# Projecting q and k of the differential layers transposed, in halves of the columns, in a four-layer decoder trunk

## What is computed

```
def diff_attention(h, w_in, w_out, lam, subln_g, cos, sin, lambda_init):
    proj = h @ w_in
    q, k, v, g = jnp.split(proj, [nq, 2 * nq, 2 * nq + DA_WIDTH], axis=-1)
    q = rope(q.reshape(B, S, 2 * H, d), cos, sin) * (d ** -0.5)
    k = rope(k.reshape(B, S, 2 * H, d), cos, sin)
    ...
        s = jnp.einsum('bhmqd,bhmkd->bhmqk', qblk, k, preferred_element_type=jnp.float32)
        p = jax.nn.softmax(jnp.where(mask, s, NEG), axis=-1)
        pd = p[:, :, 0] - lam_full * p[:, :, 1]
        return jnp.einsum('bhqk,bhkv->bhqv', pd.astype(v.dtype), v, preferred_element_type=jnp.float32)
```

## Time and profile before

| | |
|---|---|
| median of 3 runs | 1755.6 us |
| the profiled execution | 1755.62 us |
| its span | 1753.9 us |
| TensorE busy | 1745.0 us (99%) |
| VectorE busy | 1142.6 us (65%) |
| ScalarE busy | 911.0 us (52%) |
| granted TensorE clock, mean | 0.999 |

### The profile page before, as it was taken

How to read it: one execution, slowest core, us unless ns; L and a number is a source line. 1 busy time by engine, 2 the same in 40 slices (tenths; PEclk the granted TensorE clock), 3 DMA queues, 4 the chain that set the end, 5 groups by cost and what they waited for, 6 DMA issues and landing times.

```text
span 1753.9 us, 24994 instructions
## 1 busy us (share of the span) xinstructions
PE 1745.0 (99%) x8274; PEld 1458.5 (83%) x8274; DVE 1142.6 (65%) x1890; ACT 911.0 (52%) x1420; POOL 40.1 (2%) x99
## 2 busy tenths in 40 slices
PE   9999999999999999999999999999999999999998
PEld 8888888888888888888888888888888888888887
DVE  7766666665558888865655465655666666666655
ACT  7554545454556666645544444454545445454543
POOL 1000000000000000000000000000000000000000
PEclk9999999999999999999999999999999999999999
DMA  8666566655565555457997699766666666656563
GB/s 274 188 178 180 170 183 171 184 167 191 181 183 165 158 157 156 152 180 166 171 167 205 175 170 180 203 171 191 181 186 176 179 179 172 186 169 181 172 212 131
DMA packets 171300, 313.16 MB, mean 179 GB/s; under 512 B 10870, under 2 KB 27836, under 8 KB 171100
## 3 DMA queue, kind: packets, MB, share of 16 engines
q1 hardware_dynamic: 170800, 311.54, 64.8%
q0 software_dynamic: 48, 0.13, 0.2%
q10 hardware_dynamic: 380, 0.56, 0.1%
HBM read 310.10 MB, written 2.10 MB: 178 GB/s over the span
## 4 chain that ended last, share of the span: by engine, by line
PE 98%; DMA 1%; SPq 1%; DVE 0%; issue 0%; ACT 0%; POOLq 0%; POOL 0%; DVEq 0%
PE acc L957 30%; PE acc L959 30%; PE acc L958 30%; PE tp L922 4%; DMA raw<-in_da_w_in_dram 1%; PE sc L958 1%; PE sc L957 1%; PE sc L959 1%; PE sc L989 0%; PE sc L1047 0%; PE sc L1045 0%; PE sc L1046 0%; PE sc L1028 0%; PE sc L1027 0%; PE sc L1115 0%
## 5 line engine op out<-in xcount | busy, mean ns | idle before, releaser
L1770 DVE TENSOR_TENSOR w_lo<-raw,w_hi 128x1024 fp32r<-128x1024 f32 x583 | 708.1, 1223 | 463.8 <-ACT w_hi L894 462.5
L894 ACT ACTIVATE w_hi<-raw 128x1024 fp32r<-128x1024 f32 x583 | 613.5, 1058 | 456.5 <-PE acc L959 454.6
L957 PE MATMUL acc<-w_hi,xt_hi 128*128 128x512 f32 x1824 | 719.6, 394 | 0.2 <-DVE w_lo L1770 0.2
L959 PE MATMUL acc<-w_hi,xt_lo 128*128 128x512 f32 x1824 | 711.4, 390 | 0.0
L958 PE MATMUL acc<-w_lo,xt_hi 128*128 128x512 f32 x1824 | 710.3, 389 | 0.0
L959 PEld LDWEIGHTS acc<-w_hi,xt_lo 128*128 128x128 f32 x1824 | 342.3, 188 | 72.7
L958 PEld LDWEIGHTS acc<-w_lo,xt_hi 128*128 128x128 f32 x1824 | 342.8, 188 | 65.8
L957 PEld LDWEIGHTS acc<-w_hi,xt_hi 128*128 128x128 f32 x1824 | 342.6, 188 | 66.0 <-DVE w_lo L1770 0.3
L957 PE MATMUL acc<-w_hi,ot_hi 128*128 128x512 f32 (+1 forms) x520 | 202.6, 390 | 0.0
L959 PE MATMUL acc<-w_hi,ot_lo 128*128 128x512 f32 (+1 forms) x520 | 201.0, 386 | 0.0
L958 PE MATMUL acc<-w_lo,ot_hi 128*128 128x512 f32 (+1 forms) x520 | 200.7, 386 | 0.0
(11 more groups left out here) (287 smaller groups left out, 1136.6 us busy)
## 6 DMA issues: line engine op xcount, KB each, us to landing
raw<-in_da_w_in_dram SPq DMA_DIRECT2D x255, 512.0 KB, 3.7
raw<-in_ml_w_in_dram SPq DMA_DIRECT2D x96, 512.0 KB, 5.1
raw<-in_sw_w_in_dram SPq DMA_DIRECT2D x72, 512.0 KB, 3.7
raw<-in_da_w_out_dram SPq DMA_DIRECT2D x64, 512.0 KB, 3.7
raw<-in_sw_w_out_dram SPq DMA_DIRECT2D x32, 512.0 KB, 3.6
raw<-in_ml_w_in_dram SPq DMA_DIRECT2D x64, 256.0 KB, 4.5
raw<-in_ml_w_out_dram SPq DMA_DIRECT2D x32, 512.0 KB, 3.9
xres<-in_x_dram SPq DMA_DIRECT2D x3, 512.0 KB, 8.8
```

The costliest lines, as they stand in the source:

```text
L894: act.activation(w_hi[:, q:q + 2, :], raw[:, 2 * p:2 * p + 2, :], ACT.Copy).then_inc(hi_ready, 1)
L957: pe.matmul(out_ap, k_hi, m_hi, start=start, stop=False)
L959: return pe.matmul(out_ap, k_lo, m_hi, start=False, stop=stop)
L1770: dve.tensor_tensor(w_lo[:, two, :], raw[:, two, :], w_hi[:, q:q + 2, :].bitcast(F32), ALU.subtract).then_inc(lo_ready, 1)
```

## The change

In the differential layers the roles are exchanged for q and k: the weights are stationary (128 columns), and the moving operand is the x of all 256 tokens, high and low part side by side (`xt`, 512 wide) for the high part of the weights, and the high part of x alone (256 wide) for the low part. The result is q or k already transposed, heads' dimensions by tokens. The left half of a bank collects high x high and low x high, the right half high x low. ScalarE copies the right half to SBUF, and VectorE adds the left half. The job is done in two halves of 256 columns: pairs 0 to 3 hold all 2048 rows of the first half (1 KB pieces in memory), pairs 4 to 7 those of the second. The first q job of the program keeps its load order, and both halves end with pair 7.

The rotary tables are scaled by the tokens' norm factor and transposed by TensorE once per layer, since tokens now run along the row; the rotary step works on 64 partitions at a time for its cross terms. In the third layer the 256-wide fp32 score becomes three passes, with operands that are split when they are copied.

```
-ITER_EMPTIED_BY = {"da": ["act", "act", "dve", "dve"], "sw": ["act", "dve"], "ml": ["act", "dve", "act", "dve"]}
+ITER_EMPTIED_BY = {"da": ["dve", "dve", "dve", "dve"], "sw": ["act", "dve"], "ml": ["act", "dve", "act", "dve"]}
...
-DA = dict(q_evac=11, q_T=10, q_copy=14, k_evac=19, k_T=18, k_copy=22, v_evac=27,
+DA = dict(sums=(7, 11, 15, 19), table=10, table_T=8, table_copy=13, rope=(14, 16, 18, 20), split_hi=(15, 17, 19, 21),
+          split_lo=(15, 17, 19, 21), v_evac=27,
...
-        xt_hi, xt_lo = sb("xt_hi", [P, KC, S], F32R), sb("xt_lo", [P, KC, S], F32R)
+        xt = sb("xt", [P, 2, KC, S], F32R)
+        xt_hi, xt_lo = xt[:, 0], xt[:, 1]
...
+            def load_halves(w, col, J):
+
+                half = JW // 2
+                for p in range(PAIRS):
+                    sp.wait_ge(pairs_done, PAIRS * J + p + 1 - PAIRS)
+                    row, a = 4 * P * (p % 4), p // 4
+                    sp.dma_start(raw[:, 2 * p:2 * p + 2, :].rearrange("p c (b n) -> p (c b) n", b=2),
+                                 w[row:row + 4 * P, bass.ds(col + half * a, half)].rearrange("(k p) n -> p k n", p=P))\
+                      .then_inc(raw_full[p], 16)
...
-                if (i := w.due(DA["q_evac"])) is not None:
-                    evac(l, job(i, 0), i, par, qs)
...
+                for n in range(4):
+                    half, whole = n % 2, (q_whole, k_whole)[n // 2]
+                    if (i := w.due(DA["sums"][1 if w.start and n == 0 else n])) is not None:
+                        if w.start and n == 0:
+                            act.wait_ge(first_half, 1)
+                        else:
+                            act.wait_ge(pairs_done, PAIRS * job(i, n // 2) + 4 * half + 4)
...
-                if (i := w.due(DA["q_T"])) is not None:
-                    pe.wait_ge(sig["roped"], in_iter(l, "roped", i, 2))
-                    turn_eight(lambda t: qs[:, t, :], [in_iter(l, f"tp_{b}", i, 0) for b in range(2)])
-                if (i := w.due(DA["k_T"])) is not None:
-                    pe.wait_ge(sig["roped"], in_iter(l, "roped", i, 4))
-                    turn_eight(lambda t: ks[:, t, :], [in_iter(l, f"tp_{b}", i, 1) for b in range(2)])
+                if w.phase == "iter" and w.first and w.idx == DA["table_T"]:
+                    pe.wait_ge(sig["table"], in_head(l, "table", 1))
...
-                        pe.matmul(sc[h][:, 0:S], kT[:, h, 0:P], qT[:, h, :], start=True, stop=True)
+                        three(sc[h][:, 0:S], ml_k0_hi[:, h, :], ml_k0_lo[:, h, :], ml_q_hi[:, h, :], ml_q_lo[:, h, :], True, True)
...
+            def column(bank, m, k, hi, lo):
+
+                a = lambda stop: pe.matmul(acc[bank][m][:], hi, xt[:, :, k, :], start=k == 0, stop=stop)
+                b = lambda stop: pe.matmul(acc[bank][m][:, 0:S], lo, xt_hi[:, k, :], start=False, stop=False)
...
+            def pair_of_half(w, j0, j, p, par, b):
...
+                for c in range(4):
+                    k = 4 * (p % 4) + c
+                    if w.first_job_of_layer and k in (0, 12, 14):
+                        for name in ("tp_0", "tp_1") if k == 0 else ("tp_0",) if k == 12 else ("tp_1",):
+                            pe.wait_ge(free[name], in_out(w.l - 1, name, 4 if k else 3))
+                    for m in range(2):
+                        op = column(b, m, k, hi[:, c, P * m:P * m + P], lo[:, c, P * m:P * m + P])
...
+            def q_or_k_pair(w, j0, i, j, p):
+
+                par = LOOP0[w.l] % 2
+                half = p // (PAIRS // 2)
+                if p % (PAIRS // 2) == 0:
+                    if j == 1:
+                        wait_half_emptied(pe, w.l, j0 - 1, half, i)
+                    elif not w.first:
+                        wait_emptied(pe, w.l, j0 + 2 + half, i - 1)
...
+            def turn_half(s, before):
...
+                own.step(dve.tensor_tensor(a, s, cos_t, ALU.mult))
+                low, high = slice(0, 64), slice(64, P)
+                own.step(dve.tensor_tensor(b[low], s[high], sin_t[high], ALU.mult))
+                own.step(dve.tensor_tensor(b[high], s[low], sin_t[low], ALU.mult))
+                own.wait()
+                dve.tensor_tensor(s, a, b, ALU.add).then_inc(sig["roped"], 1)
...
+                        for m in range(2):
+
+                            part = whole[:, 2 * half + m, :]
+                            dve.wait_ge(sig["low_part"], in_iter(l, "low_part", i, 2 * n + m + 1))
+                            op = dve.tensor_tensor(part, part, acc[(par + half) % 2][m][:, 0:S], ALU.add)
+                        op.then_inc(dve_emptied, 1)
```

More of the change, by code:

```diff
@@ L80 @@
     "x_sq":      ((0, 0, 8), (0, 0, 8), (0, 0, 8), (0, 0, 8)),
+    "table":     ((0, 0, 0), (1, 0, 0), (0, 0, 0), (0, 0, 0)),
+    "qk_lo":     ((0, 0, 0), (0, 4, 0), (0, 0, 0), (0, 0, 0)),
+    "low_part":  ((0, 0, 0), (0, 8, 0), (0, 0, 0), (0, 0, 0)),
     "roped":     ((0, 0, 0), (0, 4, 0), (2, 2, 0), (0, 0, 0)),
@@ L407, in build, with wait_half_emptied @@
         block = ctx.enter_context(nc.Block())
+        first_half = sem("first_half")
+        def wait_half_emptied(eng, l, j, half, i):
+            eng.wait_ge(dve_emptied, emptied(l, j, i)[1] - 1 + half)
         def wait_emptied(eng, l, j, i=0):
@@ L499, in iteration @@
                                 load_first(w_in)
+                            elif j < 2:
+                                load_halves(w_in, D * j + JW * i, J + j)
                             else:
@@ L841, in side_ml @@
                 if (i := w.due(ML["qk_copy"])) is not None:
-                    take(qT[:, 0:2, :], "tp_0", tp[0][:], in_iter(l, "tp_0", i, 0))
+                    act.wait_ge(full["tp_0"], in_iter(l, "tp_0", i, 1))
+                    act.activation(ml_q_hi[:, 0:2, :], turned(0), ACT.Copy).then_inc(sig["qk_hi"], 1)
+                    act.wait_ge(full["tp_1"], in_iter(l, "tp_1", i, 1))
+                    act.activation(ml_k0_hi[:, 0:2, :], turned(1)[:, :, 0:P], ACT.Copy).then_inc(sig["qk_hi"], 1)
                 for h in range(2):
@@ L1164, in pair @@
                 if p == 0:
-                    if w.phase == "iter" and not w.first and j < 2:
+                    if w.kind == "da" and w.phase == "iter" and j == 2:
+                        wait_half_emptied(pe, w.l, j0 - 1, 0, i)
+                    elif w.phase == "iter" and not w.first and j < 2:
                         wait_emptied(pe, w.l, j0 + ITER_JOBS[w.kind] - 2, i - 1)
@@ L1447, in side_da @@
[L1447 to L1456 removed]
+                if w.phase == "iter" and w.first and w.idx == DA["table"]:
+                    dve.wait_ge(rstd_ready, 2 * l + 1)
+                    for t in range(T):
+                        scale = rstd[:, t:t + 1]
+                        halves = rope_rows[:, t].rearrange("p x (a n) -> p x a n", a=2)
+                        dve.tensor_scalar(halves[:, 0], cos_a[:, t, :].unsqueeze(1).to_broadcast([P, 2, 64]), scale, None,
+                                          ALU.mult)
+                        for a in range(2):
+                            op = dve.tensor_scalar(halves[:, 1, a], sin_a[:, t, 1 - a, :], scale, None, ALU.mult)
+                    op.then_inc(sig["table"], 1)
@@ new lines, in side_da @@
+                for n in range(4):
+                    job, half, whole = LOOP0[l] + n // 2, n % 2, (q_whole, k_whole)[n // 2]
+                    two = slice(2 * half, 2 * half + 2)
+                    at = DA["sums"][1 if w.start and n == 0 else n]
+                    if (i := w.due(at)) is not None:
+                        for m in range(2):
+                            part = whole[:, 2 * half + m, :]
+                            dve.wait_ge(sig["low_part"], in_iter(l, "low_part", i, 2 * n + m + 1))
+                            op = dve.tensor_tensor(part, part, acc[(par + half) % 2][m][:, 0:S], ALU.add)
+                        op.then_inc(dve_emptied, 1)
+                    if (i := w.due(DA["rope"][n])) is not None:
+                        if w.first:
+                            dve.wait_ge(free["sc_0"], in_head(l, "sc_0", 1))
+                        wait_half_emptied(dve, l, job, half, i)
+                        turn_half(whole[:, two, :], in_iter(l, "roped", i, n))
+                    if (i := w.due(DA["split_lo"][n])) is not None:
+                        hi, lo, src = ((q1_hi, q1_lo, q_whole[:, two, P:S]), (kT_hi, kT_lo, k_whole[:, two, :]))[n // 2]
+                        dve.wait_ge(sig["qk_hi"], in_iter(l, "qk_hi", i, n + 1))
+                        dve.tensor_tensor(lo[:, two, :], src, hi[:, two, :].bitcast(F32), ALU.subtract)\
+                           .then_inc(sig["qk_lo"], 1)
@@ L1670, in side_ml @@
                 if (i := w.due(ML["qk_copy"])) is not None:
-                    take(kT[:, 0:2, :], "tp_1", tp[1][:], in_iter(l, "tp_1", i, 0))
+                    for b, (whole, hi, lo, cols) in enumerate(((ml_q1, ml_q_hi, ml_q_lo, slice(0, S)),
```

(6 more changed lines are left out.)

117 lines of the change are left out of this document (77 added, 40 removed), and 6 rows, old and new, of the table COUNTS.

## The result

The changed kernel takes 1758.42 us (median of 20 runs, 1756.61 to 1760.66); the kernel before, on the same chip, 1755.68 us (20 runs, 1755.11 to 1757.51). The ratio is 1.0014, 95% interval 1.0008 to 1.002. So it is **slower by 2.7 us**, by less than 0.2% but with an interval that leaves no change out, where 6.5 us faster was forecast and nothing above 1752.5 was in the range.

What follows compares the result with a forecast made beforehand. TensorE was taken as the bound, busy 1745.0 of 1753.9 us. Terms -14.4 + 4.8 + 0.9 - 0.6 + 2.8 = -6.5 took 1755.6 to 1749.1 us, range 1746.0 to 1752.5.

Steps and rivals of the forecast that it cites:

- Transposes removed: Differential layers: 16 blocks of eight q and k transposes go, 0.9 us each, -14.4 us.
- Projection with the weights stationary: Differential q and k jobs: a 512-wide plus a 256-wide matmul, 0.2266 + 0.118 us, cost slightly more than before; +4.8 us.
- Rival A: q and k projections: alternating widths cost a weight load, slower from 0.128 us per 256-wide matmul, 1821 at 0.188; chance 0.06.
- The wait at the start: First k job: TensorE waits for ScalarE's copies and VectorE's adds, behind older work, to empty bank 0; +2.8 us, ends 0.4 and 4.
- Tables: Four rotary-table transposes once per differential layer, half a block each time; +0.9 us.
- third layer's scores: Third layer: 256-wide fp32 score of 0.43 us becomes three passes of 0.118, eight times; -0.6 us.
- fourth layer's start: Fourth layer's first job reads xt columns 12 to 15 already in pair 3; no cost, 1.1 us to spare.
- transfers: q and k loads come as 1 KB pieces; no cost, 10.9 us of cover.
- VectorE and ScalarE off the path: Differential iterations: VectorE gets 3.3 us more work, but neither engine delays TensorE in the steady state; no cost.
- B: No change: TensorE also waits 0.5 us per differential iteration for q's or k's halves, 4 at the start; 1754.3 us, chance 0.08.
- D: Removed transposes had covered work TensorE then waits for, half of the 14.4 comes back; 1756.3 us, chance 0.02.
- C: The wait at the first k job is absorbed as slower pairs relieve VectorE's chain; 1746.3 us, chance 0.08.

Runs made afterwards that it cites:

- all-512 version: The version with the later tables, with the low weights against both parts of x, so every q and k matmul is 512 wide; a price measurement only: 1857.35 us.
- The run with the dummies: Changed kernel with 18 unused fp32 matmuls of 128 columns ahead of TensorE's wait at the first k job: 1756.24 us.
- two and two: The version with the later tables, with both 512-wide matmuls of each k first, then both 256-wide ones: 1751.03 us.
- eight and eight: The version with the later tables, with all eight 512-wide matmuls of a pair, then its eight 256-wide ones (reversed where a half ends): 1750.91 us.
- the version with the later tables: Changed kernel with the rotary table steps moved to pairs 11 and 12 and the first half's copies and adds to pair 10: 1752.87 us.

## Why the prediction was wrong

The sign is wrong: -6.5 forecast, +2.7 measured. By its own steps:

- **Transposes removed, -14.4:** right. 1.8 per iteration fits the all-512 version to 0.05.
- **Projection with the weights stationary, +4.8:** this is the step that failed most, and by size. A unit was priced at 0.2266 + 0.118 = 0.3446 and came to 0.3515, so the term to 1024 x (0.3515 - 0.3399) = +11.9. Inside the change the 256-wide step takes 0.1167, as forecast; the 512-wide one was carried over at its price in a run of its own width, 0.2266, and takes 0.2348. In the trace of before, the 512-wide matmul behind the nine of the earlier trace rows already takes 0.23 to 0.24 to the next start (93.81 to 94.05). Prices of runs of one width would not have been enough: 0.2266 for 512 columns less 256 columns at the 2.4 GHz level, 0.1067, is 0.1199, and alone a 256-wide matmul does take 0.1200. With it the term would have been +6.8 and the forecast still -4.5. A matmul in a run of its own width costs its columns and 13 ns more, and that accounts for 2.0 of the 6.9 ns; the other 4.9 are the mixing, which no term had. The Trainium skill (TensorE: Matmul & The Clock Gate, Wait — 56ns, not 53.3ns?) puts the same form, columns over the clock plus a fixed part, with 2.5 ns for the fixed part. The form agrees with the runs of one width, the 2.5 does not: 13.3 is measured at both widths. At the lower level the Trainium skill has no fixed part in that section, and there the trace agrees: 0.42 to 0.43 and 0.21 to 0.22 in the stretch from 40.06. Rival A, that the alternation of widths costs, had the right direction; its turning point, 0.128 for the 256-wide matmul, was not reached (0.3515 - 0.2266 = 0.125, if all is put on it). Its working gives 1749.1 + 1024 x 0.0069 = 1756.2 for the unit that was measured, which is no gain against the kernel before, yet hardly slower; its end at 0.188 is out.
- **The wait at the start, +2.8:** the mechanism, the place and the chain are right, the size is not, 4.2. The run with the dummies compares best, as its sine steps stand where those of the earlier trace rows do. There the six table steps take 1.4 us (34.37 to 35.78), not 0.8; `w_lo` (1.14) and the adds (0.8) came as forecast, and the adds end at 37.7 instead of 37.0. TensorE was ready at 33.8, not 34.4. The two together are the 1.2 to 1.4 that the wait is longer. The prediction had the price of the table steps among its ends: 4 if they cost twice as much, and they cost 1.8 times.
- **What follows the wait:** missing altogether. The sum treated a wait as a delay and nothing else. The granted clock falls during it, and what comes behind pays 2.2 us more. The experiment with the dummies shows that this is the idle time's doing.
- **Tables, third layer's scores, fourth layer's start, transfers:** right, as far as they can be told apart. A score of the third layer now takes 0.36, as three steps from 875.00 to 875.36, instead of 0.43:

```profile
875.00 0.28 PE L996 MATMUL sc<-kT_hi,q_hi 128*128 128x256 f32 x1
...
875.36 0.38 PE L1155 MATMUL sc<-q,k 128*128 128x128 f32 x2
```

  From the first layer's last scores to the fourth layer's first the change gains 0.71. The terms give a gain of 0.43: the 1.8 of one iteration's transposes less 128 x 0.0116 = 1.48 for its units, less 0.45 for the tables, and 0.56 for the scores. So these terms are right within 0.3 us together. The stretches of the changed kernel that answer to the earlier trace rows:

```profile
120.00:175.00 55.00, 55.00 (x299) 47.27 (x298) 42.06 (x61) 24.87 (x36) 0.00 (x0) 1.00 0.62 184
860.00:915.00 55.00, 55.00 (x265) 46.22 (x264) 30.23 (x45) 29.54 (x43) 1.42 (x3) 1.00 0.98 161
```

- **VectorE and ScalarE off the path, rivals B and D:** no wait stands in any iteration, so B and D are out; C is out too, since the wait at the start is there.
- **The Trainium skill's rule on bare weight loads (TensorE: Matmul & The Clock Gate, The mechanism):** out, as the trace of before had it. The steps of 0.2266 in the all-512 version, with a weight load each and the weights stationary, show it for the new form too.

With the measured unit, wait and clock the sum is -14.4 + 11.9 + 0.9 - 0.6 + 4.2 + 2.2 = +4.2, against +4.8 in the profiled execution and +2.7 between the medians. Part of the 2.1 between those two is the late load at the start of the profiled execution.

By this sum the unit's miss alone takes the whole gain (-6.5 + 7.1 = +0.6), while the longer wait and the half clock alone would have left -2.9; together they make the change slower beyond the noise. With the start repaired the change is worth -2.9 us, and with two and two or eight and eight as the order -4.6 and -4.8: those versions beat both kernels. Eight and eight, at 1750.91, is the fastest that was run, and not to be told from two and two.

## What to carry to other kernels

When TensorE is never idle, price a matmul from a long run of steps, and from a run with the mix of widths that the new kernel will have, if any stands in a trace: here the prices of the two widths alone were 4.9 ns per unit short. Splitting the same columns into more matmuls is paid by the piece. A wait of several us in front of a TensorE that was busy costs more than its length, since the clock that it comes back to may be the half one: look at the granted clock behind every new wait of a profile. And before rejecting an edit that saves work in every iteration, look at the first iteration alone: here five lines of the start's schedule were worth 5.5 us, twice what the whole edit had lost.

## What the runs showed of the hardware that was not expected

- A wait of 4.2 us took TensorE to the 1.2 GHz level, and 4.8 us of work behind it went at that level; a wait of 1.2 us in the version with the later tables did not, nor did one of 3.9 us filled with dummy matmuls. With the parts of x side by side a wait of 4.1 us brought only 3.4 us of the low level, and they began 0.4 us after its end.
- In a run of one width a 512-wide matmul of the three passes starts every 0.2266 us and a 256-wide one every 0.1200 at full clock, each with a weight load of its own, for 512 whichever side is stationary: 2.4 GHz for the columns and 13.3 ns each.
- Mixing the two widths costs 1.5 to 5 ns per unit beyond that on average, by the order but not by the number of changes: least in groups of two or of eight. It does not depend on how the moving operand lies in memory; whether it depends on the roles was not tried. In turn, the same instructions run for dozens of units at 0.347 or at 0.353, and the surplus stands on the 512-wide steps (0.2348 on average), not on the 256-wide ones (0.1167).
- So the iterations of the changed kernel have two lengths, 94.5 and 94.9 us, in no order that repeats from run to run; with groups of two all six lie between 94.29 and 94.41. The runs of the change spread more too (1756.61 to 1760.66, against 1750.81 to 1752.14 in groups of two), to which the load at the start and the length of the low clock also add; the shares were not measured. What decides between the two prices was not tried.
